# Delta rule in a two-block transformer kernel: its triangular inverses from unpadded 64x64 tiles

## What is computed

```python
decay = jnp.exp(jnp.where(incl, g[..., :, None] - g[..., None, :], -jnp.inf))
m = jnp.where(strict, jnp.einsum('bhncd,bhnsd->bhncs', k_beta, k) * decay, 0.0)
t_inv = lax.linalg.triangular_solve(eye + m, eye, lower=True, unit_diagonal=True)
u = t_inv @ (v * beta);  w = t_inv @ (k_beta * exp(g))
a_intra = jnp.where(incl, jnp.einsum('bhncd,bhnsd->bhncs', q, k) * decay, 0.0)

def step(state, inp):
    v_new = u_i - w_i @ state
    o = (q_i * jnp.exp(g_i)[..., None]) @ state + a_i @ v_new
    k_dec = k_i * jnp.exp(g_last[..., None] - g_i)[..., None]
    state = state * jnp.exp(g_last) + k_dec.T @ v_new
```

## Time and profile before

| | us |
|---|---|
| median of 3 runs | 2975.66 (2973.79 to 2978.79) |
| the profiled execution, its span | 2971.8 |
| of it: block `delta_steps`, first operation to the next block | 436.4 to 847.2 |
| PE busy in the span | 2548.5 (86%) |
| DVE busy in the span | 1331.7 (45%) |
| ACT / POOL busy in the span | 742.7 (25%) / 293.0 (10%) |

### The profile page before, as it was taken

The page is one execution under the profiler, slowest core; times in us unless marked ns, Lnnn a source line. Parts: engine busy times, 40 slices in busy tenths (PEclk is TensorE's granted clock), DMA queues, the critical chain, the costliest instruction groups (busy, mean ns, idle before and its releaser), DMA issues. The chain is left out here.

```text
span 2971.8 us, 41142 instructions
## 1 busy us (share of the span) xinstructions
PE 2548.5 (86%) x17238; PEld 1886.2 (63%) x17238; DVE 1331.7 (45%) x2025; ACT 742.7 (25%) x1410; POOL 293.0 (10%) x244
## 2 busy tenths in 40 slices
PE   5999858998868879799958879956939999999998
PEld 3888636666636657588834335623828888787886
DVE  3752257777647642211056046564234434344343
ACT  3121141110023332311131155521122222132221
POOL 2000002110010022300032000005230000000000
PEclk7999969999968879799967589966969999999999
DMA  4123200000024421222300210002111111111112
GB/s 146 50 64 92 101 2 2 2 2 2 2 116 162 178 78 36 92 64 78 99 25 2 87 44 1 1 1 71 29 29 50 45 48 42 51 50 45 49 41 79
DMA packets 167091, 160.35 MB, mean 54 GB/s; under 512 B 12200, under 2 KB 146044, under 8 KB 166676
## 3 DMA queue, kind: packets, MB, share of 16 engines
q1 hardware_dynamic: 161134, 138.00, 14.6%
q0 software_dynamic: 5360, 19.92, 1.7%
q10 hardware_dynamic: 438, 0.12, 0.0%
HBM read 129.62 MB, written 28.31 MB: 53 GB/s over the span
## 5 line engine op out<-in xcount | busy, mean ns | idle before, releaser
L233 ACT ACTIVATE w_hi<-w_stage 128x1024 fp32r<-128x1024 f32 x144 | 152.3, 1057 | 686.8 <-PE proj_acc L252 226.9
L250 PE MATMUL ffn_acc<-m_hi,w_hi 128*128 128x512 f32 x704 | 274.7, 390 | 45.5 <-DVE w_lo L238 45.5
L238 DVE TENSOR_TENSOR w_lo<-w_stage,w_hi 128x1024 fp32r<-128x1024 f32 x144 | 175.4, 1219 | 257.4 <-ACT w_hi L233 257.3
L251 PE MATMUL ffn_acc<-m_lo,w_hi 128*128 128x512 f32 x704 | 274.4, 390 | 0.0
L252 PE MATMUL ffn_acc<-m_hi,w_lo 128*128 128x512 f32 x704 | 274.3, 390 | 0.0
L2531 DVE SCALAR_TENSOR_TENSOR hidden<-ffn_acc,hidden_conv,hidden 128x1023 f32<-128x1023 f32 x88 | 112.8, 1282 | 268.9 <-ACT hidden L2492 262.9
L250 PEld LDWEIGHTS ffn_acc<-m_hi,w_hi 128*128 128x128 f32 x704 | 132.5, 188 | 74.9 <-DVE w_lo L238 47.5
L250 PE MATMUL proj_acc<-m_hi,w_hi 128*128 128x512 f32 x400 | 161.7, 404 | 19.2 <-POOL m_lo L1504 19.2
L250 PE MATMUL acc<-h_hi,w_hi 128*128 128x512 f32 x432 | 169.4, 392 | 4.8 <-DVE h_lo L485 4.8
L251 PE MATMUL acc<-h_lo,w_hi 128*128 128x512 f32 x432 | 168.8, 391 | 0.0
L252 PE MATMUL acc<-h_hi,w_lo 128*128 128x512 f32 x432 | 168.7, 390 | 0.0
(11 more groups left out here) (348 smaller groups left out, 4770.1 us busy)
## 6 DMA issues: line engine op xcount, KB each, us to landing
w_stage<-in_w_in SPq DMA_DIRECT2D x48, 512.0 KB, 4.1
w_ada<-in_w_ada SPq DMA_DIRECT2D x12, 2048.0 KB, 7.9
w_stage<-in_w_up SPq DMA_DIRECT2D x44, 512.0 KB, 3.9
w_stage<-in_w_out SPq DMA_DIRECT2D x16, 512.0 KB, 4.6
conv_in<-spill SPq DMA_DIRECT2D x4, 2048.0 KB, 17.5
m_resid<-resid_spill SPq DMA_DIRECT2D x2, 4096.0 KB, 12.9
spill<-y_tok POOLq DMA_DIRECT2D x16, 512.0 KB, 4.6
w_stage<-in_w_down SPq DMA_DIRECT2D x16, 384.0 KB, 3.5
```

The costliest lines, as they stand in the source:

```text
L233: nc.scalar.activation(w_hi[:, slot], w_stage[:, slot], ACT.Copy).then_inc(w_hi_ready, 1)
L238: nc.vector.tensor_tensor(w_lo[:, slot], w_stage[:, slot], w_hi[:, slot].bitcast(F32), ALU.subtract).then_inc(w_lo_ready, 1)
L250: nc.tensor.matmul(acc[:, h, :], w_hi[:, slot, k, :], hi[:, k, tok], start=k == 0, stop=False)
L251: nc.tensor.matmul(acc[:, h, :], w_hi[:, slot, k, :], lo[:, k, tok], start=False, stop=False)
```

## The change

- **Tiles.** `key_scores`, `corner`, `inv_t` lose the zero padding. All products of the levels now take 64 rows of operands, from the half's own partitions, and write the same 64 partitions.
- **Lower triangles only.** The backward half is formed as a lower triangle too (through `key_bias`, `p_row`, `dirs` and the `join` mask). So in a level only the upper or lower halves of the blocks are computed: products stream 32 columns where they streamed 64, and `corner_mask` covers 128x128 where it covered twice 64x256. `inv_add` takes both kinds (inverse and transpose) in one operation of 128x256 in the middle levels. `inv_sum` of level 0 still streams 64.
- **`keep_busy`.** One product for a level, in a bank of its own (`idle`), also in the round that has no pair; before it was two for each step.
- **Query side.** `q_dec` and `row_decay` are gone, with the eight products of `decays` that fed them. `state_sums` forms key times state and query times state (into `kvb[0]`), ACT scales the latter by exp(g) on eviction (`q_state_scale`, 4 operations), the scores part comes into bank `kb`, DVE adds the two (L1142) and POOL stores (`store`).
- **Places.** `scale_inv` moves from DVE to POOL, in 8 operations of 64x256 for a round instead of 4 of 128x256 on DVE. The output addition of the last eight steps moves from DVE to POOL. `v_sum` does its value products first and waits for the copied key states only before the others. `gram` now waits for the last `inv_add` instead of the last `corner_mask`, since it shares the bank. `state_sums` waits for `advance` and the added output. The four memsets become two of the same total size.

```diff
-        yb = [bank(f"yb{i}", where=stS) for i in range(2)]
-        xb = [bank(f"xb{i}", (P, 2, DN_HEADS, CH), where=stS) for i in range(2)]
+        tri = [bank(f"tri{i}", where=stS) for i in range(2)]
+        pair_bank = bank("pair_bank", (P, DN_HEADS, 2, CH), stS)
+        kb = bank("kb", (P, DN_HEADS, DN_DIM), stS)
+        idle = bank("idle", where=stS)
+        ob = kvb[0]
...
                 def gram(n):
                     x = n % 2
                     if n >= 2:
-                        pe.wait_ge(s_ym[x], LEVELS * (n // 2))
+                        pe.wait_ge(s_xu[x], LEVELS * (n // 2))
...
                     for h in range(DN_HEADS):
                         for hf in range(2):
-                            mm = nc.tensor.matmul(yb[x][rows_of(hf), h * CH:(h + 1) * CH], key_scores[:, x, h, hf, :],
-                                                  inv[:, x, h, :] if lv else unit, start=True, stop=True)
+                            r = rows_of(hf)
+                            old = inv[r, x, 0, h, :] if lv else unit[r]
+                            mm = nc.tensor.matmul(tri[x][r, h * LOWER:(h + 1) * LOWER], pair_keys[r, n % 4, h, 1, :],
+                                                  lower(old, lv), start=True, stop=True)
...
-                                z = inv_t[:, x, h, hf, :] if lv else ident[:, rows_of(hf)]
-                                y = corner[:, x, h, hf, :]
-                                mm = nc.tensor.matmul(xb[x][rows_of(hf), i, h, :], y if i else z, z if i else y,
-                                                      start=True, stop=True)
+                                first = P + (kind * DN_HEADS + h) * LOWER
+                                t_old = inv[r, x, 1, h, :]
+                                mm = nc.tensor.matmul(tri[x][r, first:first + LOWER], y if kind else t_old,
+                                                      upper(t_old, lv) if kind else lower(y, lv), start=True, stop=True)
...
                     for lv in range(LEVELS):
                         if before:
-                            (k_state_sum, v_sum, out_sum)[lv % 3](before[lv // 3])
+                            (state_sums, v_sum, kv_sum)[lv % 3](before[lv // 3])
+                        if after and lv in (1, 4):
+                            pairs(after[lv // 3])
                         for n in pair:
                             corner_sum(n, lv)
-                        if after and lv in (3, 4):
-                            decays(after[lv - 3])
+                        keep_busy(idle[:, :], 1)
                         for n in pair:
-                            keep_busy(flat[n % 2])
                             inv_sum(n, lv)
...
                 def advance(n):
...
                     ins.then_inc(s_st, 1)
-                    if n >= NCH // 2:
-                        dve.wait_ge(s_osum, n + 1)
-                        for hf in range(2):
-                            c, d = side(n, hf)
-                            dst = o_dn[rows_of(hf), c // 2, :]
-                            nc.vector.tensor_tensor(dst, ob[rows_of(hf), :, :].rearrange("p a b -> p (a b)"), dst,
-                                                    ALU.add).then_inc(s_o, 1)
+                    dve.wait_ge(s_osum, n + 1)
+                    dve.wait_ge(s_qs, n + 1)
+                    nc.vector.tensor_tensor(q_state[:, n % 2], kb[:, :, :], q_state[:, n % 2], ALU.add
+                                            ).then_inc(s_oadd, 1)
```

355 lines of the change are left out of this document (182 added, 173 removed).

## The result

The changed kernel takes **2881.9 us** (median of 4 runs, 2875.64 to 2893.01) against 2974.76 for the kernel before on the same chip: a ratio of 0.969, interval 0.966 to 0.972, or 93 us less. The forecast was 3049 with a range of 2995 to 3120. It was wrong in sign: the case "the clock holds" came true, which had a chance of 0.09 and 2894 us.

A forecast was written before the change was run, and what follows sets the result against it. PE's own work bounds a round: 33.5 us, plus 21 for 1.2 GHz and 2 of waits, 56.5. Seven rounds +67.9, first +9, tail -5, setup +1.5: +73.4 on 2971.8, plus 3.9, forecast 3049 us, range 2995 to 3120.

The forecast's parts named there:

- the clock holds: Rival: PE stays at 2.4 GHz in the main loop, rounds of 37.2 us, 2894 us in all; chance 0.09.
- the price of a product: In the levels on PE: 58 ns a product, set by its weight load, whether 32 or 64 columns are streamed.
- The rival of cheaper small products: Level products at 30 ns, 7.2 us less a round, clock falling half the time: 2949 us; chance 0.08.
- The waits: PE waiting for DVE in a round: 1.1 us after level 2, 2.6 before `gram`; 3.7 in all at 2.4 GHz.
- POOL's new work: `scale_inv` on POOL, 5.8 us a round, covered by 1 to 2 us; rival that POOL is late: 3059 us, chance 0.05.
- The clock: In the rounds: small tiles let PE's clock fall in the levels, returning at dense products; granted clock 0.6 to 0.7.
- the 102 us: Stretch of a later block at clock 0.50 with PE busy 90.4 us, the forecast's weightiest evidence for a falling clock.
- That term of 21 us a round: Added to each round because 21 of PE's 33.5 us of work would run at 1.2 GHz; estimated between 0 and 33.5.
- price of 181 against 110 ns: Scan products on PE: 181 ns each in the output, where shapes take turns, 110 in groups of one shape.
- the fall behind 621.43: Old-kernel clock fall: 32 records in 3.4 us while PE waited for scores, then 3.4 us at 0.50; read as too little work.
- The first round, without a scan, at about 44 us: First round of the main loop, nearly all at 1.2 GHz: 44 us against 35.0 before, +9.
- The tail and the setup: Scan-only tail after the rounds: 30.5 us against 35.5, -5; setup ahead of the rounds: +1.5 us.

The follow-up runs named there:

- e4: Changed kernel with 64 streamed columns in the level products instead of 32 (the 32 twice); 2881.7 us.
- e17: e16 with 16 busy products added in the later block, behind the last place where PE waits for a state; 2833.4 us.
- e1: Changed kernel with no busy product in any level, the 24 at the start kept; 2889.8 us.
- e14: Changed kernel with level products of one half reading 128 rows and of the other 64, so the shape changes with every product; 3447.2 us.
- e13: Changed kernel with the later block's output products grouped by kind instead of 128-row and 64-row ones taking turns; 2873.7 us.
- e7: Kernel before the change with one busy product in each level instead of four; 2946.7 us.
- e8: Kernel before the change with output products in two groups of one shape instead of taking turns for each head; 2953.3 us.
- e12: Kernel before the change with both the edits of e7 and e8; 2929.1 us.
- e15: Changed kernel with each mask and each middle `inv_add` on DVE split into two operations of 64 rows; 2904.7 us.
- e18: e17 with the two output halves taking turns within one shape in the later block's products; 2812.1 us.
- e6: Changed kernel with the second `advance` moved behind the last `inv_add`, so that `gram` need not wait for it; 2895.4 us.
- e16: e13 with one busy product instead of 24 at the start of the delta-rule block; 2852.8 us.

## Why the prediction was wrong, point by point

**What bounds the kernel, and the price of a product: right.** 58 ns whatever the columns came out as 59 with 32 and with 64 (e4). PE's own work in a round was summed to 33.5 us; the trace has it busy 33.45. A middle level of 3.4 is 3.36. The rival of cheaper small products is refuted.

**The waits: right in place, a little large.** 2.6 us before `gram` were 1.67, and 1.1 before the state products 0.84. DVE at about 17 us a round is 16.88; POOL's new work, 11.59, is covered. The old wait for scores did go. The round at 2.4 GHz was put at 37.2 and is 37.5 with its short fall, 35.8 without.

**The clock: the step that failed.** The prediction read from the 102 us that "busy time does not hold the clock, and how much of the array works seems to", and concluded that 21 of 33.5 us would run at 1.2 GHz, in rounds of 56.5. That term of 21 us a round was measured as 1.7: a middle round is 37.47 us with one fall of 3.41 us, and 35.80 without one. Three things were wrong in the step.
- The row could not carry a statement on *holding*. It showed a clock that was down and did not come back. e17 ran these products, in groups of a kind, at 1.00 once it was up. Whether small tiles hold 2.4 GHz was not in the row, and e1 shows that they do.
- The row was not compared with the levels in the prediction's own measure. A product of the row took 0.62 us for 128 columns through 128x64 or 64x64 cells, by turns in shape; a level's product was put at 58 ns for 32 columns through 64x64. By these numbers the levels do about 1.8 times as much in a given time at 2.4 GHz as the row did, an estimate, so even by the array's work the row did not say that they fall. The prediction knew from its own price of 181 against 110 ns that turns of shape cost, and did not carry it to that row. e14 shows the clock falling under such turns, with no wait at all; the changed kernel removes them from its scan rather than adding them. The turns are not the whole of it: in e13 they are nearly gone and the clock stays at 0.50.
- It set the fall behind 621.43 beside the 102 us as one of little work in the array, when PE was waiting for scores: busy 1.55 of 3.41 us. A third old fall, at 720.41, stands behind a wait too, of 1.81 us. The falls in the changed kernel's middle rounds stand within 1.5 us of such a wait too, by turns the one before `gram` and the one before the state products. The Trainium skill (TensorE: Matmul & The Clock Gate, HAM oscillation) ties falls to idle gaps. The prediction named that and set it at 0.09; in the rounds the trace agrees in that each fall stands at a wait, though of 0.84 or 1.67 us, and not in e14, whose falls have no gap.

**Where the feared course is real.** "The first round, without a scan, at about 44 us": it took 36.15 in the profiled execution, at 0.56, and in the table 20 to 25 in those where the clock held. There it is as feared: nothing dense, a fall, no return. It was expected in the levels of every round and is there in one round of eight, in five of nine profiled executions.

**The tail and the setup.** 30.5 for the tail was 27.0; it ran at 0.94 and not at the 0.50 to 0.56 of before. The stretch ahead of the rounds was to cost 1.5 and cost 3.5.

**Where the 93 us come from**, as far as shown, each edit measured alone and therefore not exactly a share: three busy products of four 25 us (e7), output products grouped by shape 19 (e8), these two together 42 (e12), masks and additions in fewer DVE operations 17 to 23 (e15). That leaves about 28 to 34 for the decay products that are gone, the score and output waits, and the tail's clock; these were not tried one by one.

**What stays open.** Why the clock falls in the first round in some executions and not in others, with the same rows up to there. And what exactly brings it back and what holds it. Dense products of 128 rows did, and bursts of busy products, and e18's products with the halves in turn. Levels of small tiles did not in the first rounds of the changed kernel, e1 and e6, though the changed kernel has one busy product in each, while the old kernel's levels, with four, did within 3.41 us. The array's work in a given time and the time lost between shapes are both left as measures: e14 fits either, e13, e17 and e18 the first. No run was made to part them.

## What to carry to other kernels

A row in which the clock is down says nothing on whether the same work would hold it up: look for how it fell, and try one short burst of full-sized products behind the last wait before condemning the work (e17 against e16, 19 us for one burst). Compare work in a given time, and not for each product. Where products of different row counts take turns, part of PE's busy time is the change of shape: group them by shape, and within a shape let the two output halves take turns (e13, e18). And where a forecast hangs on one inference that the sum alone does not need, the case without it deserves a chance to match the evidence, here far more than 0.09.

## What the runs showed of the hardware that was not expected

- The same stream can hold the clock and be unable to bring it back. Levels of 64x64 tiles with 32 columns and no filler kept 2.4 GHz through nearly all of a round (e1, 0.91 to 0.96), but left the clock at 0.50 for 29 us when it was down. Products that write one half at a time ran 53 us at 0.50 in e13 and 28.5 us, to their end, at 1.00 in e17. With the halves in turn they brought it back at 1.2 GHz (e18, at 1506.21).
- A change of row count with every product costs twice: a product went from 59 ns to about 230 at 2.4 GHz, an estimate, and 350 at 1.2 (e14), and the clock fell although the trace shows PE busy 109.20 of 109.20 us.
- A float32 product with 128 streamed columns takes 254 ns when its neighbours write the same half, and 128 when the halves take turns (e17, e18).
- A warm-up can cost more than it gives: without the 24 busy products the block's own first products brought the clock up, and the kernel was 21 us faster (e16 against e13), in a part that is not explained: the first round kept the clock in all six profiled executions.
